# Feed-forwards: the first two output chunks of each group's second half are taken together

## The reference

```
def squared_relu_mlp(h, w1, w2):            # w1: 1024 x 4096, w2: 4096 x 1024
    return jnp.square(jax.nn.relu(h @ w1)) @ w2

x = x + g2 * rmsnorm(squared_relu_mlp(hx2, w_ff1[l], w_ff2[l]), g_post_ff[l])
```

## Time and profile before

| | |
|---|---|
| median of 3 runs | 4402.12 us |
| profiled execution | 4398.56 us |
| its span, first to last instruction | 4396.8 us |
| mean granted TensorE clock | 0.94 |
| TensorE busy | 3916.3 us |
| VectorE / ScalarE / GpSimd busy | 2095.7 / 1745.9 / 1733.5 us |

### The profile page before, as it was taken

How to read it: one execution, slowest core, us unless ns; L and a number is a source line. 1 busy time by engine, 2 the same in 40 slices (tenths; PEclk the granted TensorE clock), 3 DMA queues, 4 the chain that set the end, 5 groups by cost and what they waited for, 6 DMA issues and landing times.

```text
span 4396.8 us, 63048 instructions
## 1 busy us (share of the span) xinstructions
PE 3916.3 (89%) x22940; PEld 3190.6 (73%) x22940; DVE 2095.7 (48%) x2604; ACT 1745.9 (40%) x2893; POOL 1733.5 (39%) x928
## 2 busy tenths in 40 slices
PE   5989999899978879887999999887888888999997
PEld 4767667668656769666787878776778766887886
DVE  5446445455354326556326434636426654347225
ACT  3345354353443435454224323334334543234222
POOL 1434334334323454233444444564345233444443
PEclk8999999999989989888999999998988989999999
DMA  6423333333322230022222222343231022222233
GB/s 229 142 101 133 121 123 128 120 121 124 113 86 92 87 98 12 18 77 72 91 95 87 95 96 91 115 135 104 73 95 29 17 72 72 95 93 90 91 95 110
DMA packets 133593, 422.01 MB, mean 96 GB/s; under 512 B 16784, under 2 KB 27808, under 8 KB 132768
## 3 DMA queue, kind: packets, MB, share of 16 engines
q1 hardware_dynamic: 126352, 408.50, 28.2%
q10 hardware_dynamic: 7056, 10.97, 0.7%
HBM read 397.38 MB, written 6.29 MB: 92 GB/s over the span
## 4 chain that ended last, share of the span: by engine, by line
PE 28%; issue 27%; POOL 8%; DVE 4%; ACT 2%; DMA 1%; POOLq 0%; SPq 0%; ACTq 0%; DVEq 0%
PE lin L2403 12%; POOL wlo L1724 8%; PE lin L2407 7%; PE lin L2591 3%; PE bankT L2571 2%; PE scores L2557 1%; PE scores L2560 1%; DVE tmp L2093 1%; PE lin L2434 1%; DVE tmp L2102 1%; DVE h_lo L2113 1%; DVE a_lo L2297 1%; PE scores L2558 1%; DVE x L2131 0%; DVE h_lo L2266 0%
## 5 line engine op out<-in xcount | busy, mean ns | idle before, releaser
L1724 POOL TENSOR_TENSOR wlo<-wraw,whi 128x1024 fp32r<-128x1024 f32 x454 | 1098.2, 2421 | 1627.7 <-ACT whi L1784 1627.7
L2403 PE MATMUL lin<-h_hi,whi 128*128 128x512 f32 (+1 forms) x2016 | 773.8, 391 | 87.2 <-DVE h_lo L2113 34.0
L1784 ACT ACTIVATE whi<-wraw 128x1024 fp32r<-128x1024 f32 x454 | 477.8, 1056 | 807.0 <-PE lin L2407 575.9
L2403 PE MATMUL lin<-h_lo,whi 128*128 128x512 f32 (+1 forms) x2016 | 747.1, 378 | 0.0
L509 POOL TENSOR_TENSOR wlo<-wraw,whi 128x1024 fp32r<-128x1024 f32 x130 | 314.7, 2421 | 584.4 <-ACT whi L604 584.4
L2403 PEld LDWEIGHTS lin<-h_hi,whi 128*128 128x128 f32 x2016 | 392.4, 195 | 202.9 <-issue 86.2
L2403 PE MATMUL lin<-a_hi,whi 128*128 128x512 f32 (+1 forms) x1280 | 470.9, 375 | 51.8 <-DVE a_lo L2297 43.9
L2407 PE MATMUL lin<-h_hi,wlo 128*128 128x512 f32 (+1 forms) x2016 | 465.4, 374 | 8.5 <-POOL wlo L1724 8.4
L2403 PE MATMUL lin<-a_lo,whi 128*128 128x512 f32 (+1 forms) x1280 | 464.5, 370 | 0.0
L2403 PEld LDWEIGHTS lin<-h_lo,whi 128*128 128x128 f32 x2016 | 395.2, 196 | 67.8 <-issue 7.0
L2407 PEld LDWEIGHTS lin<-h_hi,wlo 128*128 128x128 f32 x2016 | 361.0, 193 | 80.6 <-POOL wlo L1724 15.2
(11 more groups left out here) (332 smaller groups left out, 6242.9 us busy)
## 6 DMA issues: line engine op xcount, KB each, us to landing
wraw<-in_w SPq DMA_DIRECT2D x544, 512.0 KB, 3.7
mod_ring<-in_w_ada SPq DMA_DIRECT2D x96, 512.0 KB, 4.7
mod_ring<-in_w_mod SPq DMA_DIRECT2D x32, 512.0 KB, 4.7
wraw<-in_dft_tokens SPq DMA_DIRECT2D x32, 512.0 KB, 3.2
turn<-turn SPq DMA_DIRECT2D x144, 64.0 KB, 2.1
first_ring<-in_w_mod SPq DMA_DIRECT2D x16, 512.0 KB, 17.1
q_swap<-q SPq DMA_DIRECT2D x36, 128.0 KB, 2.4
x<-in_x ACTq DMA_DIRECT2D x2, 2048.0 KB, 21.4
```

What stands on the lines that cost most here:

```text
L1724: nc.gpsimd.tensor_tensor(wlo[:, s, 0:D], wraw[:, s, 0:D], whi[:, s, 0:D].bitcast(F32), ALU.subtract)\
L1784: nc.scalar.activation(whi[:, s, 0:D], wraw[:, s, 0:D], ACT.Copy).then_inc(*w_hi.one)
L2403: nc.tensor.matmul(bank[s][:, 0:p.w], whi[:, s, k * P:(k + 1) * P], h[:, k, 0:p.w], start=(k == 0 and h is hi), stop=False)
```

## The change

The first two products of each second half (chunks g and g+1, slots and banks 0 and 1) are replaced by one function, `first_pair`. It waits first for both banks and both high weights. Then it goes through the inner blocks: for each k it waits for `a_ready`, and makes the four matmuls of both chunks with `a_hi` and `a_lo`. Then come the eight low products of chunk g and its `lin_done`, and the eight of chunk g+1 and its `lin_done`. `sum_pre` of the last group stood between the two products and now stands behind the pair. All other engines' programs are unchanged.

```diff
-                def hidden_ready(grp):
-                    return lambda k: a_ready.after(grp, k + 1)
+                def first_pair(g, grp):
+
+                    for s in range(2):
+                        pe.wait_ge(*lin_free.after(g + s, 1))
+                        pe.wait_ge(*w_hi.after(g + s, 1))
+                    for k in range(KB):
+                        pe.wait_ge(*a_ready.after(grp, k + 1))
+                        for s in range(2):
+                            for h in a_parts:
+                                nc.tensor.matmul(bank[s][:, 0:p.w], whi[:, s, k * P:(k + 1) * P], h[:, k, 0:p.w],
+                                                 start=(k == 0 and h is a_hi), stop=False)
+                    for s in range(2):
+                        pe.wait_ge(*w_split.after(g + s, 1))
+                        for k in range(KB):
+                            low = nc.tensor.matmul(bank[s][:, 0:p.w], wlo[:, s, k * P:(k + 1) * P], a_hi[:, k, 0:p.w],
+                                                   start=False, stop=(k == KB - 1))
+                        low.then_inc(*lin_done.one)
...
-                product(g0 + FF_CH, 0, p, a_parts, hidden_ready(p.it * FF_GROUPS))
-                product(g0 + FF_CH + 1, 1, p, a_parts)
+                first_pair(g0 + FF_CH, p.it * FF_GROUPS)
                 run(g0 + FF_CH, a_parts, 2)
                 with pe.Fori(1, FF_GROUPS - 1) as q_no:
                     g = q_no * (2 * FF_CH) + g0
                     run(g, h_parts, 0)
-                    product(g + FF_CH, 0, p, a_parts, hidden_ready(q_no + p.it * FF_GROUPS))
-                    product(g + (FF_CH + 1), 1, p, a_parts)
+                    first_pair(g + FF_CH, q_no + p.it * FF_GROUPS)
                     run(g + FF_CH, a_parts, 2)
                 g = g0 + (FF_GROUPS - 1) * 2 * FF_CH
                 run(g, h_parts, 0)
-                product(g + FF_CH, 0, p, a_parts, hidden_ready((p.it + 1) * FF_GROUPS - 1))
+                first_pair(g + FF_CH, (p.it + 1) * FF_GROUPS - 1)
                 if nxt:
                     sum_pre(nxt, FF_SUMS)
-                product(g + FF_CH + 1, 1, p, a_parts)
                 run(g + FF_CH, a_parts, 2)
```

## The result

| | median of the runs | ratio to the kernel before, 95% interval |
|---|---|---|
| before | 4402.3 us (6 runs) | |
| changed | 4430.51 us (6 runs, 4425.12 to 4437.93) | 1.0068 [1.0055, 1.0081] |
| changed, once more (the last experiment) | 4437.43 us | 1.008 [1.0063, 1.0096] |

The forecast was 4407, within 4397 to 4423. The time lies above the range.

The account below looks back on a forecast made before the run. TensorE, busy for 89% of the span, was taken as the bound. Terms +3.4, +0.4 and +1.2 gave +5.0 us: 4403.6 from the profiled 4398.56, or 4407 on the median (+0.11%); range 4397 to 4423.

Parts of the forecast that it names:

- The exchange of the two waits: At the sixteen 512-wide places: the wait for `a_lo` goes (26.2 us), one for g+1's weights comes (29.6 us).
- +3.4: Net us at the 512-wide places: 29.6 lost to the new wait minus 26.2 regained from the old one.
- +0.4 for the registers: Eight places inside the loop, thresholds from registers: 0.05 us taken for each, ends 0 and +1.8.
- The clock: At the new stop ahead of the pair, TensorE was taken to stay at full clock; a fall had chance 0.10.
- the rival: Clock falls at the new stop: 1.9 us a spell, 4437 at all sixteen places, 4416 at five; chance 0.10.
- The chances of "slower": Total given 0.24: 0.04 from the forecast, 0.09 from the clock falling, 0.10 from ScalarE late behind the pair.
- What it moves: Behind the pair: g+2 finds its weights, no stall, 0 us; last groups' VectorE delay caught up, at most 2.6 us per unit.
- The context: Four 256-wide context places, bound by the weights: later `lin_done` of g costs +1.2 us, ends -3 and +5.
- The rule on banks: Pair changes PSUM banks every two matmuls; by the skill page it would lose clock; the trace row speaks for no cost.

Follow-up runs that it names:

- the last experiment: The changed kernel run once more, unedited: 4437.43 us, ratio 1.008 to the kernel before.
- the wait alone: Kernel before, plus a wait for the high weights of g+1 ahead of each second half's first product, no pair: 4410.37 us, ratio 1.0035.
- two fillers: Changed kernel plus two useless matmuls per pair, into an unused bank, ahead of the wait for g+1's weights: 4415.42 us, ratio 1.0026.

## Why the prediction was wrong

**The exchange of the two waits** was right in kind: `a_lo` is not waited for at latent places; the weights of g+1 are, at all sixteen. The size was off. The terms of the sum were +3.4 and +0.4 for the registers. Where no fall comes, the changed kernel takes 0.34 us more than before to the next place at the written-out ones (89.56 against 89.22) and 0.38 inside the loop (89.71 against 89.33): 5.8 us for sixteen, against 3.8 forecast. The missing part is the way from the release to the first matmul: 0.25 us, not the 0.05 that I took over from the wait for `a_lo`. It is 0.24 inside the loop (2179.15 + 1.05 = 2180.20, to 2180.44), so the registers cost nothing there. In the kernel with the wait alone, where the released wait stands ahead of all others of the product, it is 0.05 at the written-out places; what makes the difference was not tried.

**The clock** is the step that failed. The forecast said the stop was "0.1 to 0.2 longer than one that leaves the clock alone", gave the fall a chance of 0.10, and left it out of the sum. It happened at ten of sixteen places, 1.6 us each, 16 us, more than half of the loss. Besides, the spell behind the start of the second unit became 0.9 us longer in each layer, 2 us in all, of which the forecast has nothing. The place, the price (1.9 against 1.6) and the point from which it decides (one place in four) stood in the rival; the chance was wrong, for two reasons. The idle time was taken as 1.6 us and is 1.83 to 1.95, since the release takes longer. The kernel with the wait alone has the stop of 1.63 us, and no fall behind it. And I argued from safe lengths of 1.43 and 1.54 us as if the next 0.1 to 0.4 us were safe too. The ratio of two medians with and without falls (1.0068 and 1.008 against 1.0026) gives 18 to 24 us for them. (The chances of "slower" add up to 0.23 as listed, not 0.24; nothing hangs on it.)

**What it moves** was right: g+2 finds its weights, no second stop stands behind the pair at any 512-wide place (2100.31 + 1.06 = 2101.37, g+2's first matmul at 2101.85), and the catching up of VectorE in the last groups holds, as the first stop for `h_lo` at the start of the second unit is 2.34 us idle against 2.32.

**The context** (+1.2, ends -3 and +5) is measured as +2.5, interval -1 to +7. In the two traces of the changed kernel the unit and what follows it read longer by more than that (276.6 and 276.8 us against 270.2, of which place 8 has 1.9; 712.1 and 711.9 against 704.7). How much of it is the change's is open, as the stretch from place 12 to 13 reads 702.8 to 712.1 over all these kernels.

**The rule on banks** (the Trainium skill, "TensorE: Matmul & The Clock Gate", "A second HAM failure mode: psum-queue depth-cycling") names going round the banks as what brings idle times and swings of the clock. Here the swings came, but the banks alone don't bring them: with the same going round and the stop filled there are none, and in the order of before, one bank after the other, with a longer stop there are seven.

Together: 16 (falls) + 5.8 (stops) + 2 (start of the second units) + 0.8 (the slower matmuls behind place 17) + 2.5 (context) = 27 us, where the medians say 28 and the ratio 30 [24, 36].

## What to carry to other kernels

Where two pieces of work are merged, look at which resource the second one holds when the first could already start: the merged start waits for the later of both. Start the piece that is ready, and join the other when it comes. And a stop of TensorE may cost more than its own length: where it is longer than the longest one of the same trace that left the clock alone, a spell at the lower clock may stand behind it. Here it did behind 21 of 40 such stops, so the sum should have a term for it, at about half the places.

## What the runs showed of the hardware that was not expected

- Behind single stops in an otherwise full stream of 512-wide matmuls the clock stayed at 2.4 GHz for 1.33 to 1.63 us idle (72 places in five kernels: 16 of before, 32 of the two kernels that differ from it in the context alone, 16 with two fillers, the eight written-out ones of the wait alone). It fell at some for 1.83 to 2.08 us: 10 of 16, 4 of 8 and 7 of 16. A spell is seven or eight matmuls of 0.43 us, and starts 0.3 to 1.6 us after TensorE is busy again, not with its first matmul.
- The same ten stops had a fall behind them in both traced executions of the changed kernel.
- Two matmuls without use in each of the twenty stops made a kernel 0.4% faster.
